# Twenty-three block transposes of a four-part decoder trunk taken from TensorE and given to VectorE squares and DMA

## Chip, cores and metric

One core of a Trainium2 chip runs the whole program in one launch. The metric is the device time of one execution in microseconds (us), lower is better. Three runs of the kernel before gave 2244.99, 2245.94 and 2246.2 us, median 2245.94.

## The reference

The reference is a two-layer decoder trunk on x of 256 tokens by 2048, all in float32:

```
x = x + gla_mixer(rms_norm(x) ...)            # layer 0: gated linear attention, 4 heads
x = x + swiglu(rms_norm(x), w_in, w_out)      # d_ff = 5632
k, v = shared_kv(x)                           # rms_norm, projection, k normed by head of 128
x = x + diff_attention(rms_norm(x), k, v ...) # layer 1: own queries, two softmaxes a head, 8 heads
x = x + swiglu(rms_norm(x), w_in, w_out)
```

Each of these is a product of a 256-row activation with a wide weight matrix, plus small attention products. The activation must stand with its features on the partitions to be the stationary operand of TensorE, and comes out of each product with its tokens there; so each product is followed by a transpose.

## The kernel before

The weights (about 415 MB) are streamed once. A **unit** is two 128-row slabs of a weight matrix by 512 columns (512 KB). It goes through a ring of four slots: SP (SyncE's queue) loads it into `raw`, ACT copies it to `w_hi` in the float32r form (`split`, L775), DVE subtracts to get the rest `w_lo` (`split`, L1096), and PE multiplies: twelve 128x512 matmuls, hi*hi, hi*lo and lo*hi, for two slabs and two token blocks (`unit`, L471 to L473). The activation too is kept as a hi and a lo part (`xT`, `g_oT`, `d_oT`, `xT_q`, `hT`, part 0 and part 1).

A **block** is one 512-column strip of the output: 8 units (UB) for a product over 2048, 22 units for the one over 5632 (`ffn_out`). The stages in order are gla_in (12 blocks), gla_out (4), ffn_in0 (22, as 11 pairs of blocks in a loop), ffn_out0 (4), diff_in (12), diff_out (4), ffn_in1 and ffn_out1.

The order of work is written out by hand for each engine. At **position** (b, k) each engine runs its extra jobs for that position and then its part of the stream: PE runs unit (b, k), ACT and DVE split the unit four later. The split of unit u+4 on ACT waits until PE has used unit u (`unit_used`); the load of unit u on SP waits until DVE has split unit u-4 (`lo_done`); PE waits at each unit for its lo half. So ACT and DVE have some time in hand at each position, and what they do beyond it makes PE late. Every engine's queue is in order: a job that waits holds up all behind it.

The transposes: a finished block is written with tokens on partitions, into `x` (the residual, by `x_add`, L1126), or into the staging tile `tok` (queries, keys, attention outputs). PE turns it in 8 transposes of 128x128 (`transposes`, L482, from `transpose_block`) into two PSUM banks `tps`; ACT reads these with the norm's gain into part 0 (`gained`, L785), DVE makes part 1 (`gained`, L1107). For the keys and queries one copy does (L1058, L1212). `t_done`, `t_hi`, `t_free` order this, with numbers from `transpose_jobs`.

The FFN's hidden block h goes another way: DVE multiplies it into `tok` (L1265), turns each 32x32 square of it into `scratch` (`nc.vector.transpose`, L1270), SP issues 16 DMAs of 32 KB that put the squares in their places back in `tok` (`move_squares`, L352), three ahead of each weight load, ACT copies to `hT` part 0 (`h_high`, L946) and DVE makes part 1 (`h_low`, L1276).

Of the kernel before, what the change touches and what calls it, by code (L numbers as in the profile page):

```python
# [32 lines left out]
P = 128  # L33
# [21 lines left out]
SQ = 32  # L55
# [21 lines left out]
def transpose_jobs():  # L77


    order = [("x", g, True) for g in range(4)]  # L80
    order += [("gla_qk", n, False) for n in range(4)]
    order += [("gla_o", n, True) for n in range(4)]
    order += [("gla_x", n, True) for n in range(4)]
    order += [("ffn0_x", n, True) for n in range(4)]
    for n in range(4):
        order += [("diff_k", n - 1, False)] * (n > 0) + [("x_q", n, True)]
    order += [("diff_k", 3, False), ("diff_q", 0, False)]
# [3 lines left out]
    order += [("diff_o", n, True) for n in range(4)]  # L91
    order += [("diff_x", n, True) for n in range(4)]
# [9 lines left out]
PAIR, SPLIT = transpose_jobs()  # L102

# [39 lines left out]
def trunk(nc, x_in, attn_norm, gla_w_in, w_alpha2, b_alpha, gla_head_norm, gla_w_out, kv_norm, w_kv, k_norm,  # L143
          diff_norm, diff_w_q, q_norm, lq1, lk1, lq2, lk2, diff_head_norm, diff_w_out, ffn_norm, ffn_w_in,
          ffn_w_out, const_in, out):
    with ExitStack() as ctx:
# [142 lines left out]
        h_lo = sem("h_lo")  # L289

# [11 lines left out]
        squares_in = scratch[:, :].rearrange("q (g b k t) -> q g b k t", g=P // SQ, b=TB, t=SQ)  # L302
        squares_at = tok[:, :, :].rearrange("q a n -> q (a n)").rearrange("q (s b k t) -> q s b k t", s=P // SQ, b=TB, t=SQ)
        MOVES = (P // SQ) ** 2

        def turned(tb):

            return squares_at[:, :, tb, :, :].rearrange("q s k t -> q k s t")
# [10 lines left out]
        def _(sp):  # L319
# [33 lines left out]

            def load_block(phase, b, w, col, units=UB):
                rows = w.rearrange("(u j p) n -> u p j n", j=UNIT_KT, p=P)
                for k in range(units):
                    u = UNIT0[phase] + b * units + k
                    if phase.startswith("ffn_out") and b == 0:
                        move_squares(int(phase[-1]), PAIRS - 1, k)
                    load(u % SLOTS, u, rows[k, :, :, col:col + CB], u // SLOTS)  # L360
# [6 lines left out]
            def load_pair(phase, w, i, layer=None):  # L367

                rows = w.rearrange("(u j p) (c n) -> u p j c n", j=UNIT_KT, p=P, n=CB)
                for half in range(2):  # L370
                    for k in range(UB):
                        at = half * UB + k
                        if layer is not None:
                            move_squares(layer, i - 1, at)
                        load(at % SLOTS, UNIT0[phase] + 2 * UB * i + at, rows[k, :, :, half * PAIRS + i, :], None)
# [87 lines left out]
        def _(pe):  # L463
# [114 lines left out]
            def gla_o_turn(h):  # L578
                pe.wait_ge(o_tok, h + 1)
                transpose_block(PAIR["gla_o", h], tok)  # L580
# [3 lines left out]
            for b in range(G_BLOCKS):  # L584
                for k in range(UB):
# [8 lines left out]
                    if b in (1, 2, 3, 4) and k == 2:  # L594
                        pe.wait_ge(evacuated[(b - 1) % 2], evac_count("gla_in", b - 1))
                        transpose_block(PAIR["gla_qk", b - 1], tok)
# [13 lines left out]
                    if 9 <= b and k == 5:  # L610
                        gla_o_turn(b - 9)
# [8 lines left out]
            def out_phase(phase, src, n_kt, units, x_name, before, src_jobs=None):  # L620


                for b in range(O_BLOCKS):
                    for k in range(units):
                        before(b, k)
                        if x_name and b > 0 and k == 2:
                            turn_x(phase, b - 1, x_name)
                        if k == 0:
                            acc_is_free(phase, b)
                        if b == 0 and src_jobs:  # L630
                            name, n = src_jobs
                            if k == 2 * n:
                                taken(name, n)
# [7 lines left out]
            def gla_tail(b, k):  # L641
                if b == 0 and k == 1:
                    gla_output(3)
                if b == 0 and k == 4:
                    gla_o_turn(3)

            out_phase("gla_out", g_oT, KT, UB, "gla_x", gla_tail, ("gla_o", 3))
# [12 lines left out]
            def ffn(layer, before_phase, x_name, next_name):  # L660
                phase = f"ffn_in{layer}"

                def first(half, k):
                    if half == 0 and k == 2:
# [12 lines left out]
                out_phase(f"ffn_out{layer}", hT, FKT, UBF, next_name, tail)  # L677

            ffn(0, "gla_out", "gla_x", "ffn0_x")
# [40 lines left out]
            def diff_o_turn(n):  # L720
                pe.wait_ge(o_tok, H_G + n + 1)
                transpose_block(PAIR["diff_o", n], tok)

            for b in range(D_BLOCKS):
                for k in range(UB):
                    if 6 <= b <= 9 and k == (1 if b < 9 else 0):
                        scores(2 * (b - 6) + 1)
                    if b >= 9 and k == (2 if b == 9 else 1):
                        diff_output(b - 9)
                    if b == 0 and k == 2:  # L730
# [5 lines left out]
                    if 1 <= b <= 8 and k == (4 if b < 6 else 3):  # L736
                        name = ("diff_k", b - 1) if b <= 4 else ("diff_q", b - 5)
                        pe.wait_ge(evacuated[(b - 1) % 2], evac_count("diff_in", b - 1))
                        transpose_block(PAIR[name], tok)
                    if b >= 9 and k == (6 if b == 9 else 5):  # L740
                        diff_o_turn(b - 9)
# [11 lines left out]
            def diff_tail(b, k):  # L753
                if b == 0 and k == 1:
                    diff_output(3)
                if b == 0 and k == 4:
                    diff_o_turn(3)

            out_phase("diff_out", d_oT, KT, UB, "diff_x", diff_tail, ("diff_o", 3))

            ffn(1, "diff_out", "diff_x", None)
# [5 lines left out]
        def _(act):  # L767
# [21 lines left out]
            def gained_block(name, n, dst, gain_of):  # L789
                for half in range(2):  # L790
                    kt = 4 * n + 2 * half
                    gained(half, PAIR[name, n], dst, kt, [gain_of(kt), gain_of(kt + 1)])

# [79 lines left out]
            def gla_o_high(h):  # L873
                gained_block("gla_o", h, g_oT, lambda kt: GAIN["gla_head"] + kt % (HV // P))
# [6 lines left out]
            for b in range(G_BLOCKS):  # L881
                for k in range(UB):
# [9 lines left out]
                    if k == 0 and 1 <= b <= 4:  # L892
                        if b == 1:
                            act.wait_ge(rstd_ready, 1)
                        else:
                            for half in range(2):
                                act.wait_ge(t_done[half], PAIR["gla_qk", b - 2] + 1)
# [19 lines left out]
                    if 9 <= b and k == 6:  # L917
                        gla_o_high(b - 9)
# [3 lines left out]
            def out_phase(phase, units, x_name, gain, before):  # L922
                for b in range(O_BLOCKS):
                    for k in range(units):
# [3 lines left out]
                        if x_name and b > 0 and k == 3:  # L928
# [492 lines left out]
```

## Time and profile before

| | |
|---|---|
| median of three runs | 2245.94 us |
| profiled execution, its own time | 2246.32 us |
| its span in the profile | 2244.5 us |
| busy: PE, DVE, ACT | 2233.9, 1181.2, 1047.6 us |
| DMA queue of SP | 232576 packets, 426.95 MB, 62.7% of 16 engines |

The span runs from the first to the last instruction that the profile shows; the execution's own time is 1.8 us longer. Busy time counts instructions of an engine; PE's weight loads overlap its matmuls. The rows give start and duration in us, what an engine did, and in brackets how long it had been idle and whose signal ended that.

### The profile page before, as it was taken

What the parts mean: (1) busy time and instruction counts of PE and PEld (TensorE: products, weight loads), DVE (VectorE), ACT (ScalarE), POOL (GpSimd) and SP (SyncE); (2) the same over time, 40 slices, a digit from 0 to 9 for tenths busy, and PEclk for the clock granted to TensorE, in tenths of its full rate; (3) what the DMA queues carried; (4) which work ended last, traced back from release to release, by engine and by line L of the source; (5) the groups of instructions that cost most, each with busy time, mean ns of one, the idle gap of its engine ahead of it and who ended that gap; (6) DMA issues with size and microseconds to landing.
All of it is one profiled execution on the core that took longest, in us unless ns stands there. A gap on an engine that the chain in (4) does not pass through costs nothing.

```text
span 2244.5 us, 27137 instructions
## 1 busy us (share of the span) xinstructions
PE 2233.9 (100%) x10042; PEld 1846.0 (82%) x10042; DVE 1181.2 (53%) x1288; ACT 1047.6 (47%) x1403; POOL 34.9 (2%) x62
## 2 busy tenths in 40 slices
PE   8999999999999999999999999999999999999999
PEld 7888778888888888888888888888888888888887
DVE  4555455555555555444455565555555555554443
ACT  5555444444444444444456565554444444444333
POOL 1000000000000000000001000000000000000000
PEclk9999999999999999999999999999999999999999
DMA  7555555667676676665655555566767776666665
GB/s 246 174 165 162 167 168 188 187 197 214 194 210 205 203 208 201 205 192 189 193 181 177 165 173 160 168 181 191 209 192 214 204 213 199 204 208 196 195 193 165
DMA packets 233311, 429.60 MB, mean 191 GB/s; under 512 B 18616, under 2 KB 30096, under 8 KB 233232
## 3 DMA queue, kind: packets, MB, share of 16 engines
q1 hardware_dynamic: 232576, 426.95, 62.7%
q0 software_dynamic: 384, 1.05, 0.2%
q8 instruction: 52, 0.85, 0.2%
q10 hardware_dynamic: 272, 0.52, 0.1%
q14 instruction: 27, 0.22, 0.0%
HBM read 414.82 MB, written 2.10 MB: 186 GB/s over the span
## 4 chain that ended last, share of the span: by engine, by line
PE 99%; DMA 0%; SPq 0%; DVE 0%; DVEq 0%; issue 0%
PE acc L471 32%; PE acc L473 32%; PE acc L472 32%; PE tps L482 2%; PE side L545 0%; PE side L694 0%; DMA x<-in_x 0%; PE side L532 0%; PE side L520 0%; PE side L556 0%; PE side L692 0%; PE side L716 0%; PE side L715 0%; PE side L717 0%; PE side L576 0%; PE side L575 0%
## 5 line engine op out<-in xcount | busy, mean ns | idle before, releaser
L1096 DVE TENSOR_TENSOR w_lo<-raw,w_hi 128x1024 fp32r<-128x1024 f32 x784 | 957.1, 1224 | 942.2 <-ACT w_hi L775 938.8
L775 ACT ACTIVATE w_hi<-raw 128x1024 fp32r<-128x1024 f32 x784 | 827.6, 1059 | 1065.9 <-PE acc L473 1064.1
L471 PE MATMUL acc<-w_hi,xT 128*128 128x512 f32 x2048 | 805.8, 393 | 0.1
L473 PE MATMUL acc<-w_hi,xT 128*128 128x512 f32 x2048 | 798.4, 390 | 0.0
L472 PE MATMUL acc<-w_lo,xT 128*128 128x512 f32 x2048 | 797.6, 389 | 0.0
L471 PEld LDWEIGHTS acc<-w_hi,xT 128*128 128x128 f32 x2048 | 385.1, 188 | 81.8 <-issue 2.7
L473 PEld LDWEIGHTS acc<-w_hi,xT 128*128 128x128 f32 x2048 | 384.9, 188 | 81.0
L472 PEld LDWEIGHTS acc<-w_lo,xT 128*128 128x128 f32 x2048 | 385.2, 188 | 79.9 <-issue 0.7
L471 PE MATMUL acc<-w_hi,hT 128*128 128x512 f32 x704 | 274.1, 389 | 0.0
L473 PE MATMUL acc<-w_hi,hT 128*128 128x512 f32 x704 | 273.9, 389 | 0.0
L472 PE MATMUL acc<-w_lo,hT 128*128 128x512 f32 x704 | 273.9, 389 | 0.0
L472 PEld LDWEIGHTS acc<-w_lo,hT 128*128 128x128 f32 x704 | 132.2, 188 | 27.5
L471 PEld LDWEIGHTS acc<-w_hi,hT 128*128 128x128 f32 x704 | 132.2, 188 | 27.3
L473 PEld LDWEIGHTS acc<-w_hi,hT 128*128 128x128 f32 x704 | 132.2, 188 | 27.3
L1276 DVE TENSOR_TENSOR hT<-tok,hT 128x512 f32 (+1 forms) x44 | 28.5, 689 | 77.6 <-ACT hT L946 77.6
L946 ACT ACTIVATE hT<-tok 128x512 f32 (+1 forms) x44 | 25.4, 624 | 74.5 <-DMA tok<-scratch 74.5
L471 PE MATMUL acc<-w_hi,xT_q 128*128 128x512 f32 x128 | 51.4, 402 | 0.0
L471 PE MATMUL acc<-w_hi,g_oT 128*128 128x512 f32 x128 | 50.6, 395 | 0.0
L471 PE MATMUL acc<-w_hi,d_oT 128*128 128x512 f32 x128 | 50.4, 394 | 0.0
L473 PE MATMUL acc<-w_hi,xT_q 128*128 128x512 f32 x128 | 50.0, 391 | 0.0
L473 PE MATMUL acc<-w_hi,d_oT 128*128 128x512 f32 x128 | 49.9, 390 | 0.0
L473 PE MATMUL acc<-w_hi,g_oT 128*128 128x512 f32 x128 | 49.9, 390 | 0.0
(147 smaller groups left out, 1059.0 us busy)
## 6 DMA issues: line engine op xcount, KB each, us to landing
raw<-in_ffn_w_in SPq DMA_DIRECT2D x352, 512.0 KB, 4.0
raw<-in_ffn_w_out SPq DMA_DIRECT2D x176, 512.0 KB, 4.7
raw<-in_gla_w_in SPq DMA_DIRECT2D x96, 512.0 KB, 3.8
raw<-in_w_kv SPq DMA_DIRECT2D x64, 512.0 KB, 3.7
raw<-in_gla_w_out SPq DMA_DIRECT2D x32, 512.0 KB, 4.3
raw<-in_diff_w_q SPq DMA_DIRECT2D x32, 512.0 KB, 4.3
raw<-in_diff_w_out SPq DMA_DIRECT2D x32, 512.0 KB, 3.7
tok<-scratch SPq DMA_DIRECT2D x352, 32.0 KB, 3.2
```

Source lines behind the costliest of these rows:

```text
L471: nc.tensor.matmul(acc[p][tb][:, :], hi, w_hi[:, slot, j, :], start=(kt + j == 0), stop=False)
L472: nc.tensor.matmul(acc[p][tb][:, :], hi, w_lo[:, slot, j, :], start=False, stop=False)
L473: last = nc.tensor.matmul(acc[p][tb][:, :], lo, w_hi[:, slot, j, :], start=False, stop=(kt + j == n_kt - 1))
L482: last = nc.tensor.transpose(tps[half][:, n * P:(n + 1) * P], tile, ident)
L775: nc.scalar.activation(w_hi[:, slot, :, :], raw[:, slot, :, :], ACT.Copy).then_inc(hi_done, 1)
L946: nc.scalar.activation(hidden(0, n, tb), turned(tb), ACT.Copy).then_inc(h_hi, 1)
L1096: nc.vector.tensor_tensor(w_lo[:, slot, :, :], raw[:, slot, :, :], w_hi[:, slot, :, :].bitcast(F32), ALU.subtract).then_inc(lo_done, 1)
L1276: nc.vector.tensor_tensor(hidden(1, n, tb), turned(tb), hidden(0, n, tb).bitcast(F32), ALU.subtract).then_inc(h_lo, 1)
```

## The change

23 of the 44 blocks that PE transposed are turned in the way of h: four blocks of queries and keys of layer 0 (`gla_qk`), three of four of its attention output (`gla_o`), three of four of `gla_x` (the residual for the first FFN), of `ffn0_x` (the residual for the shared keys and values), of `diff_o` and of `diff_x`, and the four blocks of shared keys (`diff_k`). The last block of gla_o, gla_x, ffn0_x, diff_o and diff_x, the input x, the queries of layer 1 (`diff_q`), their input `x_q` and the probabilities stay on PE.

For each of the 23 blocks:

- DVE turns the squares (two instructions, `turn`) at a position at = TURN_UNIT[job], mostly k = 1 of the next block, after the block stands in `x` or `tok`.
- SP issues the 16 moves from position at+8 to at+13 of its own order, three ahead of each weight load and one at the last; ahead of the first it waits for the squares.
- At position at+7 ACT waits for all 16 moves, then writes part 0 in four instructions of 128x256 (`turned_high`), and DVE makes part 1 in eight of 128x128 (`turned_low`). For `diff_k` ACT copies instead (`k_out`, two instructions of 128x512) ahead of its sums of squares (`qk_squares`); for `gla_qk` DVE does (`gla_qk_in`, two of 128x512, through the two halves of `g_v` instead of `scratch` and `tok`).
- PE waits (`turn_taken`) for blocks 1 and 2 at units 0 and 4 of the product that reads them.

```diff
+TURN_UNIT = {("gla_qk", n): UNIT0["gla_in"] + UB * (n + 1) + 1 for n in range(4)}
+TURN_UNIT.update({("gla_o", n): UNIT0["gla_in"] + UB * (9 + n) + 3 for n in range(3)})
+TURN_UNIT.update({("gla_x", n): UNIT0["gla_out"] + UB * (n + 1) + 1 for n in range(3)})
+TURN_UNIT.update({("ffn0_x", n): UNIT0["ffn_out0"] + UBF * (n + 1) + 1 for n in range(3)})
+TURN_UNIT.update({("diff_k", n): UNIT0["diff_in"] + UB * (n + 1) + 1 for n in range(4)})
+TURN_UNIT.update({("diff_o", n): UNIT0["diff_in"] + UB * (9 + n) + (4 if n == 0 else 3) for n in range(3)})
+TURN_UNIT.update({("diff_x", n): UNIT0["diff_out"] + UB * (n + 1) + 1 for n in range(3)})
...
# SP
+            def move_turned(u):
+                for (name, n), at in TURN_UNIT.items():
+                    first = MOVES_BESIDE * (u - at - TURN_MOVE)
+                    if first == 0:
+                        sp.wait_ge(turn_squares, TB * (TURN[name, n] + 1))
+                    if 0 <= first < MOVES:
+                        src, dst = (qk_in, qk_at) if name == "gla_qk" else (squares_in, squares_at)
+                        for g, s in all_moves[first:first + MOVES_BESIDE]:
+                            sp.dma_start(dst[g * SQ:(g + 1) * SQ, s], src[s * SQ:(s + 1) * SQ, g]).then_inc(turn_moved, 16)
...
# PE, the output products (one transpose_block a block goes, a wait comes)
-                        if x_name and b > 0 and k == 2:
-                            turn_x(phase, b - 1, x_name)
+                        if b == 0 and src_job:
+                            if k in (0, 4):
+                                turn_taken(src_job, 1 + (k == 4))
...
# ACT
+            def turned_high(name, n, dst, gain_of):
+                moved(name, n)
+                for k in range(4):
+                    kt = 4 * n + k
+                    last = nc.scalar.activation(tile_of(dst, 0, kt), turned_tile(k), ACT.Copy,
+                                                scale=gains[:, gain_of(kt):gain_of(kt) + 1])
+                last.then_inc(turn_hi, 1)
...
+                    if k == 0 and 2 <= b <= 5:
+                        k_out(b - 2)
                     if k == 0 and 1 <= b <= 8:
                         qk_squares(b - 1)
...
# DVE
+            def turned_low(name, n, dst, gain_of):
+                dve.wait_ge(turn_hi, TURN_SPLIT[name, n] + 1)
+                for k in range(4):
+                    kt = 4 * n + k
+                    for tb in range(TB):
+                        last = nc.vector.scalar_tensor_tensor(
+                            tile_of(dst, 1, kt)[:, tb], turned_tile(k)[:, tb], gains[:, gain_of(kt):gain_of(kt) + 1],
+                            tile_of(dst, 0, kt)[:, tb].bitcast(F32), ALU.mult, ALU.subtract)
+                last.then_inc(turn_lo, 1)
+                dve.wait_ge(turn_lo, TURN_SPLIT[name, n] + 1)
...
+                        if x_name and 0 < b and k == 1:
+                            dve.wait_ge(evacuated[(b - 1) % 2], evac_count(phase, b - 1))
+                            turn(lambda tb: x[:, tb, (b - 1) * CB:b * CB], squares_in)
...
                 def first(half, k):
                     if half == 0 and k == 0:
+                        turned_low(x_name, 2, xT, lambda kt: GAIN[gain] + kt)
                         x_add(before_phase, 3, UB)
...
             def gla_tail(b, k):
                 if b == 0 and k == 2:
+                    turned_low("gla_o", 2, g_oT, gla_o_gain)
                     gla_o_out(3)
...
             def qk_norm(n):
+                if 1 <= n <= 4:
+                    dve.wait_ge(k_turned, n)
...
+                if n < 4:
+                    dve.wait_ge(evacuated[n % 2], evac_count("diff_in", n))
+                    turn(lambda tb: tok[:, tb, :], squares_in)
```

## Rows read from the trace of the kernel before

**Rows 1.** The page, part 1: busy us (share) and instructions.
```profile
PE 2233.9 (100%) x10042; PEld 1846.0 (82%) x10042; DVE 1181.2 (53%) x1288; ACT 1047.6 (47%) x1403; POOL 34.9 (2%) x62
```

**Rows 2.** Waits: who waited for whom, us in total, times, longest.
```profile
ACT w_hi L775 <- PE acc L473: 1064.1, 666, 4.3
```

**Rows 3.** The chain in order of time: start, us, what; gla_out.
```profile
346.84 0.87 PE tps L482 x8
369.50 0.87 PE tps L482 x8
```

**Rows 4.** Timeline of ACT in two FFN pairs.
```profile
600.75 1.06 ACT L775 ACTIVATE w_hi<-raw 128x1024 fp32r<-128x1024 f32 x1 [1.66 <-PE acc L473]
603.47 1.06 ACT L775 ACTIVATE w_hi<-raw 128x1024 fp32r<-128x1024 f32 x1 [1.66 <-PE acc L473]
608.05 1.15 ACT L946 ACTIVATE hT<-tok 128x512 f32 x2 [3.52 <-DMA tok<-scratch]
...
1632.78 1.15 ACT L946 ACTIVATE hT<-tok 128x512 f32 x2 [2.99 <-DMA tok<-scratch]
```

**Rows 5.** Timeline of SP's queue in the FFN pairs: moves of h.
```profile
603.67 0.51 SPq L352 DMA_DIRECT2D tok<-scratch  x1
...
634.71 1.79 SPq L352 DMA_DIRECT2D tok<-scratch  x3
...
647.19 0.51 SPq L352 DMA_DIRECT2D tok<-scratch  x1
...
1628.93 0.51 SPq L352 DMA_DIRECT2D tok<-scratch  x1
```

**Rows 6.** Timeline of DVE in an FFN pair: squares of h.
```profile
631.63 1.30 DVE L1270 STREAM_TRANSPOSE scratch<-tok 128x512 f32<-128x512 f32 x2
```

**Rows 7.** Groups by line and shape: count, busy us, mean ns of one.
```profile
L946 ACT ACTIVATE hT<-tok 128x512 f32 x40 | 23.1, 624 | 68.2 <-DMA tok<-scratch 68.2
L891 ACT ACTIVATE a_w<-a_raw 128x256 fp32r<-128x256 f32 x1 | 0.4, 401 | 0.0
L1165 DVE SCALAR_TENSOR_TENSOR g_q<-g_q,scratch 128x128 f32<-128x128 f32 x16 | 4.7, 292 | 0.5
```

**Rows 8.** Timeline of ACT and DVE in diff_in, block 0 ending.
```profile
1154.79 1.06 ACT L775 ACTIVATE w_hi<-raw 128x1024 fp32r<-128x1024 f32 x1 [0.21 <-PE acc L473]
...
1158.49 1.09 ACT L775 ACTIVATE w_hi<-raw 128x1024 fp32r<-128x1024 f32 x1
...
1160.95 1.29 DVE L1325 TENSOR_TENSOR tok<-acc,g_rstd 128x512 f32<-128x512 f32 x2
```

**Rows 9.** Timeline of POOL at the same place.
```profile
1160.72 0.20 POOL L450 TENSOR_TENSOR g_rstd<-g_inv,rstd 128x8 f32<-128x8 f32 x1
```

**Rows 10.** Timeline of DVE in gla_out, block 0 ending (E at 341.44).
```profile
343.73 1.28 DVE L1126 TENSOR_TENSOR x<-acc,x 128x512 f32<-128x512 f32 x2
```

**Rows 11.** Timeline of ACT, DVE and PE in gla_in, block 9.
```profile
249.40 0.58 ACT L801 ACTIVATE junk<-side 128x512 f32<-128x512 f32 x1
...
251.15 1.06 ACT L775 ACTIVATE w_hi<-raw 128x1024 fp32r<-128x1024 f32 x1 [0.37 <-PE acc L473]
...
253.39 1.40 DVE L1189 SCALAR_TENSOR_TENSOR tok<-side,o_rstd,g_r 128x512 f32<-128x512 f32 x2
...
242.85 1.02 PE L574 MATMUL side<-g_v,g_at 128*128 128x512 f32 x2
...
268.11 1.02 PE L574 MATMUL side<-g_v,g_at 128*128 128x512 f32 x2
```

**Rows 12.** The page, part 6: issues, KB each, median us from issue to landing.
```profile
tok<-scratch SPq DMA_DIRECT2D x352, 32.0 KB, 3.2
```

**Rows 13.** Timeline of PE after the first loads.
```profile
11.46 0.63 PE L471 MATMUL acc<-w_hi,xT 128*128 128x512 f32 x1
11.89 0.63 PE L472 MATMUL acc<-w_lo,xT 128*128 128x512 f32 x1
```

**Rows 14.** The same stretch by windows: busy us of PE, PEld, DVE, ACT, POOL, then PEclk, DMA, GB/s.
```profile
10.00:20.00 10.00, 9.96 (x39) 8.11 (x40) 6.43 (x11) 5.91 (x10) 5.10 (x8) 1.00 1.05 361
```

More of the change, by code:

```diff
@@ L80, in transpose_jobs @@
     order = [("x", g, True) for g in range(4)]
[L81 to L87, printed above, removed]
+    order += [("gla_o", 3, True), ("gla_x", 3, True), ("ffn0_x", 3, True)]
+    order += [("x_q", n, True) for n in range(4)]
+    order += [("diff_q", 0, False)]
     for n in range(1, 4):
@@ L90, in transpose_jobs @@
     order += [("probs", 3, False)]
-    order += [("diff_o", n, True) for n in range(4)]
-    order += [("diff_x", n, True) for n in range(4)]
+    order += [("diff_o", 3, True), ("diff_x", 3, True)]
     pair, split = {}, {}
@@ L644, in gla_tail @@
                 if b == 0 and k == 4:
-                    gla_o_turn(3)
-            out_phase("gla_out", g_oT, KT, UB, "gla_x", gla_tail, ("gla_o", 3))
+                    gla_o_turn()
+            out_phase("gla_out", g_oT, KT, UB, gla_tail, "gla_o")
             def ffn_pair(layer, i, jobs):
@@ L729, in _ @@
                         diff_output(b - 9)
+                    if b == 0 and k == 0:
+                        turn_taken("ffn0_x", 2)
                     if b == 0 and k == 2:
@@ L756, in diff_tail @@
                 if b == 0 and k == 4:
-                    diff_o_turn(3)
-            out_phase("diff_out", d_oT, KT, UB, "diff_x", diff_tail, ("diff_o", 3))
-            ffn(1, "diff_out", "diff_x", None)
+                    diff_o_turn()
+            out_phase("diff_out", d_oT, KT, UB, diff_tail, "diff_o")
+            ffn(1, "diff_out", "diff_x")
         @block.scalar
@@ L895, in _ @@
                         else:
-                            for half in range(2):
-                                act.wait_ge(t_done[half], PAIR["gla_qk", b - 2] + 1)
+                            act.wait_ge(turn_squares, TB * (TURN["gla_qk", b - 2] + 1))
                         block_out("gla_in", b - 1, lambda tb: tok[:, tb, :])
@@ L927, in out_phase @@
                             x_squares(phase, b - 1)
-                        if x_name and b > 0 and k == 3:
-                            gained_block(x_name, b - 1, xT, lambda kt: GAIN[gain] + kt)
+                        for n in range(3):
+                            if x_name and b * units + k == (n + 1) * units + 8:
+                                turned_high(x_name, n, xT, lambda kt: GAIN[gain] + kt)
                         split_ahead(UNIT0[phase] + b * units + k)
@@ L965, in first @@
                 def first(half, k):
+                    if half == 0 and k == 0:
+                        turned_high(x_name, 2, xT, lambda kt: GAIN[gain] + kt)
                     if half == 0 and k == 1:
@@ L1245, in out_phase @@
                             x_add(phase, b - 1, units)
-                        if x_name and b > 0 and k == 3:
-                            gained_block(x_name, b - 1, xT, lambda kt: GAIN[gain] + kt)
+                        if x_name and 0 < b and k == 1:
+                            if b == 1 and phase in ("gla_out", "diff_out"):
+                                tok_is_free(PAIR[f"{phase[:-4]}_o", 3])
+                            dve.wait_ge(evacuated[(b - 1) % 2], evac_count(phase, b - 1))
+                            turn(lambda tb: x[:, tb, (b - 1) * CB:b * CB], squares_in)
+                        for n in range(3):
+                            if x_name and b * units + k == (n + 1) * units + 8:
+                                turned_low(x_name, n, xT, lambda kt: GAIN[gain] + kt)
                         split_ahead(UNIT0[phase] + b * units + k)
@@ L1295, in first @@
                         x_sum(n_sum)
-                    if half == 1 and k == 7:
-                        tok_is_free(PAIR[("gla_o", "diff_o")[layer], 3])
                 ffn_pair(layer, 0, first)
```

174 lines of the change are left out of this document (108 added, 66 removed).

## Prediction, made before the changed kernel ran

> **What bounds the kernel now.** I read the page first: PE is busy for 2233.9 of 2244.5 us, while DVE and ACT are busy for about half [rows 1]. The waits say the same from the other side: ACT waits 1064.1 us in all for PE to give up a weight slot, never much the other way [rows 2]. So each microsecond of work that leaves PE shortens the kernel, unless it brings a moment at which PE waits; and work on ACT, DVE and SP is free as long as the weight splits and what PE reads come in time. The prediction is therefore a gain that is easy to count, less waits that must be worked out site by site.
>
> **The pace.** ACT's splits follow each other at 603.47 - 600.75 = 2.72 us [rows 4]: that is one unit on PE, twelve matmuls, 0.227 us each. ACT starts a split about 0.05 us after PE ends a unit; I call that end E. The next unit's extra jobs start on ACT at E+1.1 and on DVE at E+2.4. The unit that is being split is needed three units later, at E+4x2.72 = E+10.9 counted from the end of the unit before its position. That is the whole cover.
>
> **What leaves PE.** From one transposed block to the next in gla_out is 369.50 - 346.84 = 22.66 us [rows 3]; eight units are 21.76. A block's eight transposes thus cost 0.90 us (the rows call 0.87 of it transposes, the rest is the change of shape). 23 x 0.90 = 20.7 us. It lies on the path that sets the end in full, so 20.7 us is the gain if nothing waits.
>
> **What it adds.** The chain for one block is: squares, 16 moves, landing, ACT, DVE. The squares take 1.30 us [rows 6]. In the FFN SP takes from 634.71 to 647.19+0.51 = 12.99 us to issue the 16 moves with five weight loads between them [rows 5]: SP is bound by itself there. After the last issue ended, ACT started 608.05-(603.67+0.51) = 3.87 us later, and in another pair 1632.78-(1628.93+0.51) = 3.34 us later [rows 4, 5]. I take 3.65. With 0.15 for the signal to SP, 16.8 us pass from the end of the squares to ACT's release (16.5 to 17.0 by the two ends). The part 0 step is four 128x256 copies out of SBUF: one such ran 0.40, two of 128x512 take 1.15 [rows 4, 7], so 1.4 with overlap (bounds 1.15 and 1.6). Part 1 is eight of 128x128 at 0.29 each [rows 7]; overlapped some 0.21 apart, 1.8 with its own wait (bounds 1.65 and 2.3).
>
> The transfer page would make this shorter: the Trainium skill, "DMA: Bandwidth & Descriptors" (its latency part), puts a DMA at about 2.0 us plus its bytes over 436 GB/s, some 2.1 us for 32 KB. By that the chain would be about 15.2 us and the result near 2232; the trace's 3.34 and 3.87 disagree, and I go by them.
>
> Site by site, times from the block's end E or from E', the end of the unit before the squares' position:
>
> *gla_qk* (4). The squares end at E'+3.7, release at about E'+21; DVE alone waits, at a position it would start at E'+21.4. The copy and next squares are 2.6 us. No wait of PE. *ffn0_x* (3): blocks are 22 units long and the consumer has no haste. None.
>
> *gla_x, diff_x* (3 each). At k=0 x_add runs at E+2.3 for 1.28 [rows 10], then a split, then the squares at k=1 end at E'+3.7. SP's last move must follow a load that waits for a split at E'+16, so it ends at E'+17.2 and the release is E'+20.8, just after ACT is free (E'+20.2). Then 1.4 + 1.8 + a split 1.15 + squares 1.3 + signals 0.1 = 5.75: the second block's squares end at 20.8+5.75-21.76 = E'+4.8, release 21.6; the third's at 5.6, release 22.4. No split is late. But the third is taken at unit 0 of the FFN, and `x_add` of the last block stands behind `turned_low` on DVE. It ends at 22.4+1.4+1.8+1.28+0.1 = E'+27.0, and PE, in order, asks for it at unit 2 to transpose that block, at 9 x 2.72 = E'+24.5. PE waits 2.5 us; twice, 5.0. Behind PE's wait stand all its units.
>
> *gla_o, diff_o* (3 each). Blocks here last 268.11-242.85 = 25.26 with their transposes [rows 11], 24.4 without; the side products take 2.6. The product starts at E'+2.3 for 1.4 [rows 11], squares end at E'+5.0, then 6.9 from the second on, since ACT has its sums of squares first (two of 0.58 with a readout each, the first at 249.40, the split behind them by 251.15 in rows 11; here they end at E'+24.0) and `turned_high` follows. The third release is at E'+23.7; +1.4+1.8+1.4+0.1 gives `gla_o_out(3)` done at 28.4, where PE at unit 4 wants it at 24.5+2.6 = 27.1. 1.3 us, and I take the same for diff_o: 2.6.
>
> *diff_k* (4). This is the largest. Now ACT starts the squares sums as soon as the split is through: split 1154.79 (E = 1154.74), next split at 1158.49, so about 2.75 lie between for the eight sums; POOL's last factor starts at 1160.72, and behind it DVE's `qk_norm` runs 1160.95 to 1162.24, E+7.5 [rows 8, 9]. With squares behind it, E+8.9. The release is 16.8 later, E+25.7 = 3.0 after the next block's end (22.66 with the `x_q` transposes). There `k_out` (1.2) stands ahead of the sums, so they end at E+7.2, and the next squares at E+3.0+9.1 = E+12.1: all splits still just in time (needed at 10.9 and 13.6, done at 9.3 and 13.3). One block on, release is 12.1+16.8-22.66 = E+6.2: the split of unit 4 is done at 12.5 (needed 10.9), and the one of unit 5, behind `qk_norm` and squares, at 16.5 (needed 15.2): 2.9 us. The loop from squares to squares is 16.8+9.1 = 25.9 us, longer than PE's 22.66, so the next costs 3.2. In block 5 release comes at E+7.5, and PE wants `qk_norm(4)` for its own transposes at unit 4: done 15.2, wanted 10.9, 4.3 us. Together 10.4.
>
> Each wait also loses PE's overlap of weight load and matmul, about 0.2 us for each of nine: 1.8.
>
> SP's 368 more issues, 0.59 us each, ahead of weight loads: in the FFN the same three fit a unit, 2.47 of 2.72 us. The latest squares, of diff_k, end at E'+12.6; the load behind the first three moves is issued by 15 and lands by 19, its split is through at 21, and PE wants it at 8 x 2.72 = 21.8 plus the 2.9 it has waited. Nothing; if that cover went, a late load would be a wait as long as it is late.
>
> **Sum.** 20.7 - (10.4 + 5.0 + 2.6) - 1.8 = 0.9 us gained. Against the profiled execution's own time, 2246.3 - 0.9 = 2245.4 us. That execution is 0.4 above the median of the runs.
>
> **Rivals.** (1) *The waits are much smaller*: the loops are only just longer than PE's, so little takes them away. The page's median landing is 3.2 from the start of an issue, 2.7 from its end, 0.95 under what I took [rows 12], and the two steps' lower ends give 0.4. Priced with a release 1.5 us earlier, some 4.1 stay in diff_k, 0.5 at the x and 0.7 at the o sites, 1.0 of restarts: gain 14.4, 2232. For it: each site's wait grows out of differences of 1 to 3 us between long sums, and the moves may find a less busy DMA than in the FFN. Against: 22 waits of ACT for these moves [rows 7], 68.2 us in 20 of them, 3.4 each, hardly vary. With no wait at all, 2225.6. 0.29.
>
> (2) *The release is later by 1 us or so* (landing, larger strided costs, loads that come late): diff_k +3.6, x sites +6 as it adds up over three blocks, o sites +2: 2257. It decides from about 0.4 us on. For it: the moves share the queue with loads bunched behind a late wait. 0.14.
>
> (3) *The clock falls in the new waits*: early in the run, after PE had been idle, matmuls came 11.89-11.46 = 0.43 us apart instead of 0.227, the lower of the two levels (1.2 and 2.4 GHz), though the granted clock is put at 1.00 there [rows 13, 14]. That stretch was ten matmuls, 2 us lost. At five waits of 2.5 us and more this is +10: 2255. From one such fall on, two more; with three the result is slower. Against: in all of the rest PE never waited, so no row shows it. 0.12.
> The Trainium skill, "TensorE: Matmul & The Clock Gate" (HAM oscillation), warns of idle gaps like the one of 4.3 us in block 5; the trace of before has none to check it by.
>
> (4) Forecast, the sum as it stands, within 5 us: 0.45.
>
> **Chances and range.** A time under 2241.8 is faster by over 0.2%, over 2250.8 slower; 0.2% is about what a measurement of this kernel tells from no change. Faster: case 1 and 0.04 of the forecast, 0.33. Slower: cases 2 and 3, 0.26. Same 0.41. The range takes in case 1 and most of 2 and 3: 2231 to 2256; the forecast's own range, by the bounds of landing and the two steps, is 2239 to 2251.
>
> **What would show it.** After: no more than 21 blocks of transposes on L482; PE idle in front of units 4 and 5 of blocks 3 and 4 of diff_in waiting for `w_lo`, in front of a `tok` transpose in block 5, in front of the `x` transposes at the start of both FFNs for `x_add`, and in front of `tok` transposes in gla_out and diff_out. ACT's wait for `tok<-scratch` growing from block to block in diff_in. If PE's idle sum is near 11 us as before, the waits were a mistake and the time is near 2226; if matmuls come 0.43 us apart behind a wait, case 3.

## The result, and the profile after

The changed kernel takes 2264.03 us, the median of four runs (2260.84 to 2267.17), against 2246.07 (2244.99 to 2246.25) for the kernel before: a ratio of 1.0081, 95% interval 1.0068 to 1.0094. It is 0.8% slower, and the time lies outside the range. The profiled execution took 2260.84 us with a span of 2259.1 (before 2246.32 and 2244.5), so 14.6 us of span have to be explained. Its mean granted clock is 0.995, where before it was 1.000.

The page of the kernel after, parts 1, 4 and 6. In part 1 the columns are those of [rows 1]; part 4 is the chain that ended last, by engine:

```profile
PE 2222.9 (98%) x9858; PEld 1831.8 (81%) x9858; DVE 1215.3 (54%) x1394; ACT 1049.3 (46%) x1403; POOL 35.0 (2%) x62
...
PE 88%; SPq 4%; DVE 4%; DMA 3%; ACT 1%; issue 1%; POOL 0%; DVEq 0%; ACTq 0%; POOLq 0%
...
tok<-scratch SPq DMA_DIRECT2D x656, 32.0 KB, 3.1
```

PE issues 184 instructions fewer (23 x 8) and is busy 11.0 us less, not 20.7, while the span has grown. Its idle time went from 10.6 to 36.2 us. And 12% of the chain now runs over other engines, SP's queue, DVE and the moves first among them. The waits after (in total, times, longest; L843 and L1076 are the ACT copies `turned_high` and `k_out`, L1161 is DVE's weight split, L1209 `x_add`, L524 a transpose, L513 the first matmul of a product):

```profile
ACT xT L843 <- DMA tok<-scratch: 21.6, 9, 4.2
...
ACT d_k L1076 <- DMA tok<-scratch: 14.3, 4, 4.5
...
PE tps L524 <- DVE x L1209: 10.1, 2, 5.9
...
PE acc L513 <- DVE w_lo L1161: 5.9, 4, 2.8
```

Two more of PE's waits, 3.5 and 3.1 us, stand in front of the `tok` transposes of the two attention outputs, and one of 3.3 in front of those of the first queries. These are the places that the prediction named. By stage, from the start of each stage's first matmul in the two traces (the change of a stage's length = saving + waits + slow clock + rest). A wait here is the time from the start of one matmul to the start of the next, less the usual 0.227 us, so it holds what the restart loses. Slow clock is what the matmuls and transposes behind a wait lie further apart than at the higher clock level:

| stage | change | saving | waits of PE | slow clock |
|---|---|---|---|---|
| gla_in (gla_qk, gla_o) | -6.1 | -6.3 | | |
| gla_out | +3.5 | -2.7 | 3.6 | 2.6 |
| ffn_in0 | +7.5 | | 6.1 | 1.5 |
| ffn_out0 | -2.7 | -2.7 | | |
| diff_in, keys | +1.2 | -2.7 | 3.5 | |
| diff_in, queries | +7.3 | -0.9 | 6.4 | 1.8 |
| diff_in, values (diff_o) | -2.7 | -2.7 | | |
| diff_out | +0.8 | -2.7 | 3.3 | |
| ffn_in1 | +6.0 | | 4.4 | 1.7 |
| all | +14.6 | -20.7 | 27.2 | 7.5 |

PE waits 27.2 us more, where the sum had 19.8 (18.0, and 1.8 for the restarts). Idle time alone, as the brackets of the timelines give it, is 25.8 of the 27.2. The slow clock is a term that the sum did not have at all. 0.6 us is left over.

**The largest site, the start of the first FFN.** Timelines of the kernel after: DVE's squares of `x`, ACT and DVE at the third block, PE.

```profile
346.36 1.30 DVE L1185 STREAM_TRANSPOSE scratch<-x 128x512 f32<-128x512 f32 x2
...
370.34 1.30 DVE L1185 STREAM_TRANSPOSE scratch<-x 128x512 f32<-128x512 f32 x2
...
394.41 1.30 DVE L1185 STREAM_TRANSPOSE scratch<-x 128x512 f32<-128x512 f32 x2
```
```profile
365.23 1.71 ACT L843 ACTIVATE xT<-tok,gains 128x256 fp32r<-128x256 f32 x4 [1.02 <-DMA tok<-scratch]
...
389.30 1.71 ACT L843 ACTIVATE xT<-tok,gains 128x256 fp32r<-128x256 f32 x4 [3.32 <-DMA tok<-scratch]
...
412.64 1.70 ACT L843 ACTIVATE xT<-tok,gains 128x256 fp32r<-128x256 f32 x4 [4.24 <-DMA tok<-scratch]
```
```profile
414.38 2.19 DVE L1194 SCALAR_TENSOR_TENSOR xT<-tok,gains,xT 128x128 fp32r<-128x128 f32 x8 [4.72 <-ACT xT L843]
416.60 1.29 DVE L1209 TENSOR_TENSOR x<-acc,x 128x512 f32<-128x512 f32 x2
```
```profile
411.63 0.39 PE L515 MATMUL acc<-w_hi,xT 128*128 128x512 f32 x1
417.95 1.97 PE L524 MATMUL tps<-const,x 128*128 128x128 f32 x8 [5.93 <-DVE x L1209]
419.57 0.78 PE L513 MATMUL acc<-w_hi,xT 128*128 128x512 f32 x1
420.14 0.63 PE L514 MATMUL acc<-w_lo,xT 128*128 128x512 f32 x1
420.57 0.57 PE L515 MATMUL acc<-w_hi,xT 128*128 128x512 f32 x1
```

The squares follow each other after 23.98 and 24.07 us, where PE needs 21.76 for eight units. So each loop adds over 2 us of delay. ACT's wait grows from 1.02 to 4.24 us. `x_add` (L1209) stands behind the third part 1 and ends at 417.89, 5.9 us after PE's last matmul. PE resumes with transposes of 1.97 us (0.87 in [rows 3]) and matmuls that start 0.43 to 0.57 us apart until 421. Windows of that place (us, busy of PE, PEld, DVE, ACT, POOL, then PEclk, DMA, GB/s):

```profile
412.00:418.00 6.00, 0.07 (x2) 0.06 (x1) 3.58 (x11) 2.72 (x6) 0.00 (x0) 0.68 0.48 159
418.00:421.00 3.00, 3.00 (x12) 2.73 (x13) 1.64 (x2) 2.32 (x5) 0.00 (x0) 0.51 0.29 53
421.00:432.00 11.00, 11.00 (x50) 9.10 (x49) 5.85 (x9) 5.17 (x8) 0.89 (x2) 1.00 0.54 176
```

The granted clock is 0.51 in the 3 us behind this wait: the lower of the two levels (1.2 of 2.4 GHz). In the kernel before, the profile puts it at 1.00 up to the last microsecond.

**The shared keys.** Timeline of ACT after, blocks 2 to 4 of diff_in:

```profile
1183.16 1.34 ACT L1076 ACTIVATE d_k<-tok,gains 128x512 f32<-128x512 f32 x2 [2.63 <-DMA tok<-scratch]
...
1209.04 1.34 ACT L1076 ACTIVATE d_k<-tok,gains 128x512 f32<-128x512 f32 x2 [3.84 <-DMA tok<-scratch]
...
1235.98 1.34 ACT L1076 ACTIVATE d_k<-tok,gains 128x512 f32<-128x512 f32 x2 [4.54 <-DMA tok<-scratch]
```
ACT's wait for `tok<-scratch` grows over these three blocks; the fourth, at 1261.50, waits 3.30. DVE's squares, at 1164.28, 1190.94, 1216.81 and 1243.75, are 26.7, 25.9 and 26.9 us apart, a mean of 26.5: the loop that the prediction put at 25.9 us and set against PE's 22.66.

### The profile page after: what moved, and what is told of

The parts are those of the page before. It is cut to its first block, busy times and chain, and to the rows that moved or that the text cites. A ratio compares the mean times of both kernels' runs of the same rounds, so it can differ in the third digit from the quotient of the medians.

```text
span 2259.1 us, 27233 instructions
## 1 busy us (share of the span) xinstructions
PE 2222.9 (98%) x9858; PEld 1831.8 (81%) x9858; DVE 1215.3 (54%) x1394; ACT 1049.3 (46%) x1403; POOL 35.0 (2%) x62
## 4 chain that ended last, share of the span: by engine, by line
PE 88%; SPq 4%; DVE 4%; DMA 3%; ACT 1%; issue 1%; POOL 0%; DVEq 0%; ACTq 0%; POOLq 0%
PE acc L513 28%; PE acc L515 28%; PE acc L514 28%; SPq L391 3%; DMA tok<-scratch 2%; DVE w_lo L1161 2%; SPq L369 1%; PE tps L524 1%; ACT junk L1096 0%; DVE scratch L1185 0%; PE side L587 0%; DVE xT L1194 0%; PE side L736 0%; DMA x<-in_x 0%; POOL g_inv L474 0%
## 5 line engine op out<-in xcount | busy, mean ns | idle before, releaser
L1161 DVE TENSOR_TENSOR w_lo<-raw,w_hi 128x1024 fp32r<-128x1024 f32 x784 | 954.2, 1223 | 894.5 <-ACT w_hi L816 890.4
L513 PE MATMUL acc<-w_hi,xT 128*128 128x512 f32 x2048 | 805.9, 394 | 3.0 <-DVE w_lo L1161 3.0
L513 PEld LDWEIGHTS acc<-w_hi,xT 128*128 128x128 f32 x2048 | 385.7, 188 | 86.4 <-DVE w_lo L1161 4.3
L513 PE MATMUL acc<-w_hi,hT 128*128 128x512 f32 x704 | 273.9, 389 | 0.0
L513 PEld LDWEIGHTS acc<-w_hi,hT 128*128 128x128 f32 x704 | 132.1, 188 | 27.6
L1377 DVE TENSOR_TENSOR hT<-tok,hT 128x512 f32 (+1 forms) x44 | 28.5, 689 | 71.1 <-ACT hT L1001 71.1
L513 PE MATMUL acc<-w_hi,xT_q 128*128 128x512 f32 x128 | 52.1, 407 | 2.8 <-DVE w_lo L1161 2.8
L513 PE MATMUL acc<-w_hi,g_oT 128*128 128x512 f32 x128 | 51.1, 399 | 0.0
L514 PE MATMUL acc<-w_lo,g_oT 128*128 128x512 f32 x128 | 50.5, 395 | 0.0
L514 PE MATMUL acc<-w_lo,xT_q 128*128 128x512 f32 x128 | 50.4, 394 | 0.0
```

Source lines behind the costliest of these rows:

```text
L513: nc.tensor.matmul(acc[p][tb][:, :], hi, w_hi[:, slot, j, :], start=(kt + j == 0), stop=False)
L514: nc.tensor.matmul(acc[p][tb][:, :], hi, w_lo[:, slot, j, :], start=False, stop=False)
L1161: nc.vector.tensor_tensor(w_lo[:, slot, :, :], raw[:, slot, :, :], w_hi[:, slot, :, :].bitcast(F32), ALU.subtract).then_inc(lo_done, 1)
L1377: nc.vector.tensor_tensor(hidden(1, n, tb), turned(tb), hidden(0, n, tb).bitcast(F32), ALU.subtract).then_inc(h_lo, 1)
```

## The experiments

Their times are medians, each beside runs of the kernel before on the same chip. The theory A: the orders on DVE and ACT at the two kinds of site put PE behind a wait for moves, and each such wait also costs clock. The rivals: B, weight loads that come late because the moves stand ahead of them; C, a price on every turned block, wherever it stands.

### Two orders

**e1**: `x_add` goes ahead of the part 1 that waits.
```diff
                     if half == 0 and k == 0:
-                        turned_low(x_name, 2, xT, lambda kt: GAIN[gain] + kt)
                         x_add(before_phase, 3, UB)
+                        turned_low(x_name, 2, xT, lambda kt: GAIN[gain] + kt)
```


> The changed kernel with one order turned round: at the start of both FFNs DVE runs x_add of the last block ahead of turned_low of the third. Theory A (a few in-order waits behind the chain squares, 16 moves, landing, copies): the two waits of PE for x_add, 6.1 and 4.4 us in the trace, go, and with them the slow matmuls and transposes behind them, 1.6 and 1.8 us: about 14 us off, near 2250 us. Rival B (weight loads that land late, bunched behind the moves, are what makes PE late): that order does nothing for the loads, the time stays near 2264.

Measured: 2251.69 us, ratio 1.0024 (1.0014 to 1.0033). The first FFN's stage is 0.41 us longer than before, not 7.54, and the second's 0.21, not 6.02. PE's waits for `x` are gone. The waits in diff_in stay.

**e2**: the sums of squares go ahead of the copy of the keys.
```diff
-                    if k == 0 and 2 <= b <= 5:
-                        k_out(b - 2)
                     if k == 0 and 1 <= b <= 8:
                         qk_squares(b - 1)
+                    if k == 0 and 2 <= b <= 5:
+                        k_out(b - 2)
```


> The changed kernel with k_out behind qk_squares on ACT in diff_in, so that the sums of squares no longer wait for the moves. Theory A: the loop from squares to squares loses the 2.9 us of sums and 2.3 us of POOL and falls under PE's period of 22.7 us, so the five waits in blocks 2 to 5 (9.9 us) and the slow stretch in block 4 (1.7 us) go: near 2252 us. Rival B (late weight loads): ACT's waits for the weights of that stage stay, and PE's with them: over 2260 us.

Measured: 2250.37 us, 1.0022 (1.0011 to 1.0034). The key blocks are 2.72 us shorter than before and the query blocks 0.95: the whole saving, with none of the five waits. The timeline of ACT in e2, at the copy of the second block of keys:

```profile
1207.15 0.24 ACT L1096 ACTIVATION_READ_ACCUMULATOR junk<-acc,rstd 128x1 f32 x1
1207.50 1.34 ACT L1076 ACTIVATE d_k<-tok,gains 128x512 f32<-128x512 f32 x2
1208.74 1.99 ACT L816 ACTIVATE w_hi<-raw 128x1024 fp32r<-128x1024 f32 x2
```

The copy follows its sums without a noted wait for the moves (of the four copies one shows such a wait, 0.45 us). The loop is cut: the squares no longer stand behind the copy that stands behind the moves, and they follow each other at PE's pace (1189.53 and 1212.28, 22.75 apart).

### Fewer blocks

**e3**: the third block of the four sites with a border behind it stays on PE, 19 are turned. The rest of the edit, not shown, brings back PE's transposes for a block that is not turned; e5, e6 and e7 are built on it.
```diff
+ON_PE = [("diff_o", 2), ("diff_x", 2), ("gla_o", 2), ("gla_x", 2)]
+TURN_UNIT = {job: at for job, at in TURN_UNIT.items() if job not in ON_PE}
```


> The third blocks of gla_o, gla_x, diff_o and diff_x are transposed by PE again, 19 blocks are still turned. Theory A: the four waits at the phase borders go, 3.6 + 6.1 + 3.3 + 4.4 us, and three slow stretches of 2.7, 1.6 and 1.8 us; four blocks cost 3.6 us of PE again: about 20 us off, near 2244 us. Rival C (each turned block costs some time on its own, by contention of moves and loads or more work for ACT and DVE): (18 + 20.7) / 23 = 1.7 us a block, so 4 blocks off give 2.8 us net: 2261.

Measured: 2245.53 us, 0.9996 (0.9986 to 1.0006). PE's border waits are gone, those of diff_in stay: 18.5 us for giving four blocks back.

**e7**: only gla_qk and ffn0_x are turned, seven blocks.
```diff
+TURN_UNIT = {job: at for job, at in TURN_UNIT.items() if job[0] in ("gla_qk", "ffn0_x")}
```


> One part of the change alone: only the four blocks of gla_qk and the three of ffn0_x are turned, where the prediction saw no wait of PE. Theory A: 7 x 0.90 = 6.3 us less than before, 2239.8. Rival C (a price on each turned block): at least 5 us over before.

Measured: 2239.83 us, 0.9972 (0.9962 to 0.9983). 6.3 us for seven blocks is 0.90 each, the whole of what a block's transposes cost, so C falls for these seven. For all 23 it is bounded by e9, below.

**e5**: e2 and e3 together.


> The two repairs that keep most turned blocks: the third blocks of gla_o, gla_x, diff_o and diff_x on PE, and k_out behind the sums of squares; 19 blocks are turned. Theory A: 19 x 0.90 = 17.1 us less than before and only the two waits of about 1 us left that the run with the thirds on PE shows in blocks 11: near 2231 us, faster than the kernel before by 0.7%. Rival C (a price on each turned block): 19 x (1.7 - 0.9) = 15 us slower than before, 2261, or with the two repairs taken as independent, 2232.

Measured: 2234.28 us, 0.9946 (0.9933 to 0.996), 3 us more than expected. The trace has the two waits that were foreseen, 0.8 and 1.2 us, and a third of 1.6 us in front of the transposes of the first queries, which was not.

**e6**: both orders of e1 and e2, with only the third block of gla_o and of diff_o back on PE, 21 turned.


> 21 blocks turned: x_add first at both FFN starts, k_out behind the sums of squares, and only the thirds of gla_o and diff_o on PE. Theory A: 21 x 0.90 = 18.9 us less, about 2 us of waits in blocks 11: near 2229 us, some 2 us under the run with 19. If turned_low for the third x block comes too late for unit 4 of the FFN, 1 to 3 us of that is lost: 2230 to 2232.

Measured: 2234.01 us, 0.9945 (0.9931 to 0.9958): no better than e5 beyond the intervals, 5 us more than expected, though the lowest run is at 2230.05. The execution at 2230.05 is the one that was profiled, and its trace has only the two waits that were foreseen, 1.1 and 1.2 us. What the others lose, no trace shows.

### The clock by itself

**e4**: 18 matmuls of 128x512 into a bank that nobody reads, in front of the transposes at the start of each FFN. They fill most of PE's wait; the computation is unchanged.
```diff
                     if half == 0 and k == 2:
+                        for n in range(18):
+                            nc.tensor.matmul(side[0][:, :], xT[:, 0, n % 4, 0:P], xT[:, 0, 0:2, :], start=True, stop=True)
                         turn_x(before_phase, 3, x_name)
```


> The changed kernel with 18 matmuls of 128x512 more at the start of each FFN, into a PSUM bank that nothing reads, ahead of PE's wait for x_add: they fill 4.1 of the 6.1 and 4.4 us that PE is idle there, and nothing else changes. Theory A with the clock as a part of the price: no matmuls 0.43 us apart behind these two waits, 3.3 us less, near 2260.7. If the clock is no matter of these waits: the same time as the changed kernel, or later where the matmuls outlast the wait.

Measured: 2261.06 us, 1.0062 (1.0045 to 1.0079). Its interval overlaps that of the changed kernel, so the trace has to decide. PE and then the windows of e4 at the same place:

```profile
412.07 4.24 PE L708 MATMUL side<-xT 128*128 128x512 f32 x18
417.44 1.09 PE L524 MATMUL tps<-const,x 128*128 128x128 f32 x8 [1.12 <-DVE x L1211]
418.29 0.48 PE L513 MATMUL acc<-w_hi,xT 128*128 128x512 f32 x1
418.61 0.39 PE L514 MATMUL acc<-w_lo,xT 128*128 128x512 f32 x1
```
```profile
412.00:418.00 6.00, 4.88 (x25) 3.79 (x24) 4.10 (x11) 3.24 (x7) 0.00 (x0) 1.00 0.24 89
418.00:421.00 3.00, 3.00 (x17) 2.54 (x16) 1.64 (x2) 1.81 (x5) 0.00 (x0) 1.00 0.43 107
```

PE resumes as late as it did (417.44), but the clock is 1.00 where it was 0.51, and 17 matmuls and transposes fall into the 3 us where 12 did. The stage is 2.1 us shorter than in the changed kernel. So this part of the loss, 1.5 us by the table, is the clock's and not the wait's. At the second FFN no fall of the clock follows either, but there PE resumes 1.9 us later behind its last unit than in the changed kernel, and the stage is 0.3 us longer: the total says little, the evidence is the clock in the trace. The other two falls of e4 (at the attention output and in the queries) are where nothing was filled in.

### The queue of moves

**e8**: four moves ahead of each load in place of three, so that three loads stand among the 16 moves and not five. All 23 blocks are turned, both orders as in the change.
```diff
+TURN_BESIDE = 4
...
-                    first = MOVES_BESIDE * (u - at - TURN_MOVE)
+                    first = TURN_BESIDE * (u - at - TURN_MOVE)
...
-                        for g, s in all_moves[first:first + MOVES_BESIDE]:
+                        for g, s in all_moves[first:first + TURN_BESIDE]:
```


> The changed kernel with four of its moves ahead of each weight load instead of three (those of h as before): three loads lie between the 16 moves instead of five, so the last move is issued 1.2 us earlier behind late squares. Theory A: each wait of the chain shrinks by 1.2 to 3 us where it adds up over blocks, together some 10 us of the 27, fewer slow stretches: 2250 to 2255. Rival B (the weight loads behind the moves are what comes late): with more moves ahead of each load, PE waits longer: over 2266.

Measured: 2235.53 us, 0.9956 (0.994 to 0.9971): 28.5 us off the changed kernel for one number, 14 to 20 more than I had expected. B says that more moves ahead of a load must make it worse; it falls. Loads do come late for ACT: in the changed kernel it waits 43.8 us in all for `raw`, where it waited 1.6 before. But in e9, below, it waits 45.5 us for them, and there PE never waits for a weight. Timelines of SP's queue and of ACT in e8, the first `x` block of gla_out:

```profile
343.22 2.42 SPq L392 DMA_DIRECT2D tok<-scratch  x4
...
351.85 0.58 SPq L370 DMA_DIRECT2D raw<-in_gla_w_out  x1
352.47 2.41 SPq L392 DMA_DIRECT2D tok<-scratch  x4
```
```profile
359.67 1.70 ACT L844 ACTIVATE xT<-tok,gains 128x256 fp32r<-128x256 f32 x4
```

The 16 moves are issued by 354.88, 11.66 us from the start of the first (13.31 in the changed kernel, from 347.68 to 360.99, below), and ACT finds them landed: no bracket. Nor does it wait at the second and third block.

**e10**: the moves in groups of 3, 3, 3, 3 and 4: the sixteenth is no longer alone behind a load of its own.
```diff
-                    if 0 <= first < MOVES:
+                    if 0 <= first < MOVES - 1:
...
-                        for g, s in all_moves[first:first + MOVES_BESIDE]:
+                        for g, s in all_moves[first:first + MOVES_BESIDE + (first == 12)]:
```


> The changed kernel with its moves 3, 3, 3, 3 and 4 ahead of five loads, so the sixteenth is no longer issued alone behind the fifth load; nothing else changes. Theory A with the landing as the mis-sized term (the lone move stands in the queues behind 512 KB that were issued just ahead of it): the release comes 2 us or more earlier, as with four moves ahead of each load, and most waits of PE go: 2236 to 2242 us. If only the time of issue counts (one load's 0.6 us earlier): 2255 to 2260.

Measured: 2240.15 us, 0.9975 (0.9965 to 0.9984), 23.9 us off for moving one DMA per block. Timelines of SP's queue at the end of a block's moves, first the kernel after, then e10, and e10's ACT:

```profile
347.68 1.78 SPq L391 DMA_DIRECT2D tok<-scratch  x3
...
357.76 1.77 SPq L391 DMA_DIRECT2D tok<-scratch  x3
360.06 0.37 SPq L369 DMA_DIRECT2D raw<-in_gla_w_out  x1
360.48 0.51 SPq L391 DMA_DIRECT2D tok<-scratch  x1
```
```profile
344.28 1.78 SPq L391 DMA_DIRECT2D tok<-scratch  x3
...
353.94 0.37 SPq L369 DMA_DIRECT2D raw<-in_gla_w_out  x1
354.36 2.41 SPq L391 DMA_DIRECT2D tok<-scratch  x4
```
```profile
360.72 1.70 ACT L843 ACTIVATE xT<-tok,gains 128x256 fp32r<-128x256 f32 x4
...
1174.49 1.34 ACT L1076 ACTIVATE d_k<-tok,gains 128x512 f32<-128x512 f32 x2 [0.57 <-DMA tok<-scratch]
...
1198.92 1.34 ACT L1076 ACTIVATE d_k<-tok,gains 128x512 f32<-128x512 f32 x2 [2.16 <-DMA tok<-scratch]
```

In the changed kernel it took, from the end of the last issue to ACT's start, 4.24, 4.89 and 3.16 us at the three `x` blocks of gla_out and 3.54, 3.24, 3.92 and 3.69 at the four key blocks, a mean of 3.81. In e10 the two `x` blocks and the four key blocks at which ACT's wait shows it give 3.03, 3.09, 2.47, 2.55, 2.97 and 3.25, a mean of 2.89. So the lone move behind its load costs 0.9 us of landing, and one load less among the moves 0.6 of issue: at the keys the release comes 15.6 us after the squares (mean of four), not 17.2. That is 1.6 us earlier, where I expected 2 or more. The landings themselves say the same over all 23 blocks: from the end of the last issue to the last landing 3.79 us on average in the changed kernel and 2.89 in e10, while the moves of h, whose last one stays alone behind a load in both, take 3.26 and 3.64. But the place behind the load is not all of it: in e8, where the last move is also the fourth behind a load, it is 2.19. I have not separated what the fewer loads among the moves do there. ACT's waits for the moves of `x`, 21.6 us in nine before, are in e10:

```profile
ACT xT L843 <- DMA tok<-scratch: 3.2, 4, 1.5
```

**e9**: e8 with both orders of e1 and e2, all 23 blocks turned.


> All 23 blocks turned, four of their moves ahead of each load, x_add first at both FFN starts and k_out behind the sums of squares. Theory A: 20.7 us less than before and, of the waits in the run with four moves alone, those in diff_in (1.9) and at the FFN starts (1.1 each) gone, while those for side products and tok transposes in the two output products (1.1 to 1.4 each, about five) stay: near 2231 us, at or a little under the run with 21 blocks (2234).

Measured: 2231.75 us (2231.11 to 2233.45), 0.9938 (0.9924 to 0.9951), the lowest median, though its interval overlaps those of e5 and e6: 14.2 us off the kernel before, of 20.7. Its mean granted clock is 1.000. The waits of PE that the kernel before lacks are 1.7, 1.0 and 0.9 us at `tok` transposes and 1.8 at side products that wait for ACT's `d_v` and `g_v`, 5.4 of the 6.5 us that are missing. So little is left for a price on every turned block (C).

## Why the prediction was wrong

*What bounds the kernel, and what leaves PE*: right. The three stages in which PE does not wait are shorter by 0.9 us a block, and e7 measures 0.90.

*gla_qk and ffn0_x, no wait*: right; -6.1 and -2.7 us by stage.

*diff_k, 10.4*: right in mechanism and size. PE waited 3.5 and 6.4 us in the two parts, 9.9 in all; the loop was 25.9 to 26.9 us by the squares, and e2 took all of it away by cutting the loop. The loop was 0.6 us longer than forecast and the waits no longer; the last release came early, 16.45 us behind its squares, and the rest is not accounted for, so the size is in part luck.

*The landing, 3.65, and with it 16.8 to the release*: **too short, the first of the two steps that failed.** It is a term mis-sized, and the waits of 18.0 us became 25.8 by it and by the two steps that follow. From the squares' end to ACT's start it took 17.57, 17.66 and 16.93 us at gla_x and 17.58, 16.80, 17.86 and 16.45 at the keys, a mean of 17.3 for 16.8. Of the 0.5 us the landing has 0.15 (3.81 for 3.65) and the issues 0.3: groups of three moves that took up to 2.95 us and not 1.78, and SP's waits in between. *The steps, 1.4 and 1.8*: 1.71 and 2.19, near the upper bounds. I had the bounds and took the middle. These are not 0.5 us once. In a loop longer than PE's period each round adds them again. At `gla_x`: 0.77 + 0.86 + 0.13 from the three releases, 0.66 + 0.66 from release to next squares (6.41 us for 5.75), 0.65 from the last release to the end of `x_add` (5.25 for 4.6). That is 3.7 us, and PE waited 5.93 where 2.5 was forecast. At gla_o the third squares end 0.9 us later than the sum has them, the release takes 0.6 longer and the way from it to the end of the product 0.7; gla_o and diff_o waited 3.6 and 3.3 for 1.3. This was rival 2, "decides from about 0.4 us on". It held at the x and the o sites and not at the keys, with a release later by 0.5 us and not by 1, and I gave it 0.14.

*The restarts, 1.8 us*: **this is the step that failed outright.** The sum priced a wait of 3 us as 3 us and 0.2 for the start. The start itself was right (27.2 less 25.8 is 1.4 us for nine waits, 0.16 each); that the clock stays up behind a wait was not. In the trace four waits are followed by a stretch at the lower level, 2.6, 1.5, 1.8 and 1.7 us lost. That was rival 3, priced at 2 each, close to what it cost, but taken as an alternative at 0.12. It is no alternative: it comes with the waits of the forecast itself. The forecast of 2245.4 with the prices of both rivals on top, 11.6 and 10, is 2267 us, where the range ended at 2256. In e4 the clock stays at 1.00 with PE filled, in e9 with no wait above 1.7 us.

The Trainium skill, "TensorE: Matmul & The Clock Gate" (HAM oscillation), warns of idle gaps, and I set it aside because the trace of before had no gap to check it by. That was a misreading: it has one of 5.28 us at its start, and the eight transposes behind it take 1.97 us, as they do behind the waits of after, though the profile puts the granted clock at 1.00 there:

```profile
5.28 0.25 PE L502 MATMUL side<-const,gain_rows 16*128 16x16 f32 x1 [5.28 <-DMA gain_rows<-in_gla_attn_norm]
5.47 1.97 PE L482 MATMUL tps<-const,x 128*128 128x128 f32 x8
```

The trace of after agrees that gaps of 3.5 and 5.9 us bring the clock down, and shows too that it is not each gap of some 3 us.

*The sum*: 19.8 for waits and restarts became 27.2, and 7.5 came for the clock. With the 0.6 left over that is the 15.5 us between 0.9 gained and 14.6 lost in the profiled execution. The other three runs are 2 to 6 us slower still. More falls of the clock would do that, but it is not shown: their mean granted clocks are 0.995, 0.995 and 0.993, where the profiled one has 0.995, so that for two of them the clock tells no difference.

*SP's issues ahead of the loads, nothing*: right as a cost to PE: ACT waits for late loads, PE does not (e9). But the question was put the wrong way round. What mattered was what a load does to the move behind it. I read 3.34 and 3.87 off the FFN and took them for what a landing takes; they were already the time of a lone move behind a 512 KB load. The Trainium skill, "DMA: Bandwidth & Descriptors" (Anatomy of one DMA), gives about 2.0 us plus the bytes over 436 GB/s, fitted on DMAs issued from GpSimd; the estimate from it for 32 KB is 2.1 us. These moves are issued from SP. The 2.47 to 3.25 of e10, counted from the end of an issue, come nearer to it than the 3.16 to 4.89 of the changed kernel; the mean of 2.19 in e8 is about there.

*Rival 1, waits much smaller*: wrong for this kernel, and nearly what e8 became, 2235.53 for its 2232: its condition, a release 1.5 us earlier, can be had by how the moves are grouped (e10, 1.6 us at the keys).

Left open: why the clock fell after some waits of about 3 us and not after others; why it stayed down longer after some than after others (in e2, after a wait of 6.23 us at the first FFN, for 6 us, where the changed kernel has 3); and why e1, e2 and e3, which gain 12.3, 13.7 and 18.5 us against the changed kernel, end in e5 and e6 some 3 to 5 us short of what was expected, beyond the 1.6 us in the trace of e5.

## What to carry to other kernels

A chain taken off the bounding engine is free only while the whole loop, from issue to reuse, is shorter than that engine's period for the same block; once it is longer, each error of half a microsecond counts once per round, so cut the loop (put what others wait for ahead of what waits for a DMA) before trusting the sum. Price a wait of PE with the clock that it may bring down. In a queue that carries large loads, look at what the last small transfer of a group stands behind: here one DMA per block, moved ahead of a load, was worth 24 us, because the loops were only just longer than PE's period.

## What the runs showed of the hardware

- A 32 KB move issued alone right behind a 512 KB load on the same queue reached its reader 3.16 to 4.89 us after its issue ended; as the last of four behind a load, 2.47 to 3.25 us. By the landings over 23 blocks the means are 3.79 and 2.89 us, and 2.19 as the last of four with three loads among the 16 moves (e8). Over 23 blocks the landing and the earlier issue made 23.9 us in e10.
- The clock after a wait of PE: transposes of 1.97 us for eight in place of 0.87, after waits of 3.45 and 5.93 us (0.50 and 0.51 granted). After 2.83 us at a `w_lo` the fall came 1.2 us after PE had resumed; after 3.26 us it did not come. Over the traces of the changed kernel and of e1 to e10, behind the start, PE has 22 waits of 2.5 us and more: 16 go with a stretch at the lower level, the shortest of them 2.50 us (e10), and 6 do not, the longest of them 3.64 us (e1). None of the 6 waits of 1.5 to 2.1 us goes with one. Timeline of PE after, three of these:

```profile
326.68 1.97 PE L524 MATMUL tps<-const,tok 128*128 128x128 f32 x8 [3.45 <-DVE tok L1273]
...
1242.36 0.50 PE L513 MATMUL acc<-w_hi,xT_q 128*128 128x512 f32 x1 [2.83 <-DVE w_lo L1161]
...
1244.11 0.63 PE L513 MATMUL acc<-w_hi,xT_q 128*128 128x512 f32 x1
...
1269.29 1.09 PE L524 MATMUL tps<-const,tok 128*128 128x128 f32 x8 [3.26 <-DVE tok L1426]
...
1270.45 0.39 PE L514 MATMUL acc<-w_lo,xT_q 128*128 128x512 f32 x1
```

- DVE's eight 128x128 pieces out of the turned squares took 2.19 us. One of them takes 0.35 us and one of ACT's 128x256 0.50, where [rows 7] has 0.29 and 0.40 for single instructions of these shapes on other tiles. ACT's four 128x256 took 1.71 us, where two of 128x512, as many elements, took 1.34.
